# A PEER decoder block: the first product of tokens 0-511 in two passes over U, two token tiles each

## The chip, the cores and the metric

The kernel runs on one core of a Trainium2 chip. The metric is the device time of one execution in microseconds (us), from the first instruction to the last with the launch around them. All arithmetic that counts for the tables is done in float32, a value split into a high part (fp32r) and a low part.

## The reference, cut to what matters

One decoder layer over 1024 tokens of width 1024: attention and a convolution side by side, then a feed-forward part that looks experts up by product keys. The second part is what the change touches.

```python
q = (xb @ w_q).reshape(T, 8, 2, 128)             # 8 heads, two halves
s = einsum('thpc,hpkc->thpk', q, sub_keys)       # 128 keys for each half
top_s, top_i = top_k(s, 16)                      # 16 of 128, then the 16 best sums of pairs
...
ids = i1 * 128 + i2                              # 8 x 16 = 128 experts of 16384 for each token
g = softmax(best_s)
act = gelu(einsum('td,thkd->thk', xb, u_tab[ids]))
y = einsum('thk,thkd->td', g * act, v_tab[ids])  # then h + y, and a last norm
```

## The kernel before, in words

P = 128, D = 1024, DK = 8 chunks of the width, tokens in NT = 8 tiles of 128, HALF = 512 tokens = HT = 4 tiles. TensorE is PE, VectorE DVE, ScalarE ACT, GpSimd POOL, SyncE SP. Every engine's program is written out by hand and kept in order by counting semaphores; nothing is reordered at run time.

The first 785 us (mixing part, queries, key scores and their top 16) are the same in both kernels. Three stages follow.

**First product.** Tokens 0-511 are multiplied with all 16384 rows of U. U comes in NB = 32 blocks of 512 experts, each in two halves `hb` of KH = 4 chunks. For a half, SP loads 1 MB (`xraw<-in_uX`, L316, two slots), ACT rounds it (`hx`, L636), DVE takes the rest (`lx`, L1049), and PE does 4 chunks x 4 tiles x 3 products (L1426). After a block ACT copies four banks to `hst` (L642) and SP stores them to the DRAM tensor `hidden` (L322, 256 KB each). `load_x(hb)` waits for `lx_ready` of two halves earlier, and stands in SP's queue behind the stores of the block before. `high_u` waits until PE is through with the half two before.

Beside the first half of the blocks DVE finds the experts (`pick`, 14 steps for each of 8 tiles, PICK_STEPS = 4 steps for each half). PE turns the result of tiles 4-7 (L1403). Beside the second half the gates of tokens 512-1023 are spread out to a dense 128 x 128 matrix for each token, in 64 blocks of 8 tokens, two for each half: DVE `mark` (L1058), ACT `plain` (L669) and POOL `scale_hot` (L427) make one-hot operands, PE multiplies them (L1413, 16 small matmuls), ACT copies (`gather`, L662), SP writes `gates`, 16 times 2 MB (L326).

**Boundary.** Then POOL gathers from `hidden` the values that tokens 0-511 chose (L437, one instruction for each of the 512 columns), ACT applies Gelu (L709), DVE multiplies with the gate.

**Groups.** Tokens 512-1023 are computed densely over all experts, in NG = 32 groups of 4 blocks of 128 experts: first product (L1454, 96 matmuls, operands `uh`, `ul` from `u_raw`), Gelu (L730), times gate (L1121), second product (L1462, 96 matmuls), added to `acc` (L1141). For tokens 0-511 POOL gathers one row of V for each of the 512 columns (`gather_row`, L449, 512 KB, a ring of VS = 8 slots) and DVE adds it (`combine`, L1106), 16 rows in each group. POOL's order in a group is 8 rows, then 8 pairs of row and value, then 8 values:

```python
for c in range(NG):
    for j in range(PER_GROUP + VS):
        if j < PER_GROUP:
            gather_row(c * PER_GROUP + j)
        if j >= VS and c + 2 < NG:
            gather_value(c + 2, j - VS)
```

Of the kernel before, what the change touches and what calls it, by code (L numbers as in the profile page):

```python
# [5 lines left out]
P = 128  # L6
D = 1024
T = 1024
DK = D // P
# [24 lines left out]
BANKS = 4  # L34
# [9 lines left out]
PICK_STEPS = 4  # L44
PICKED = list(range(NT // 2, NT)) + list(range(NT // 2))
TURN_AT = [STEPS_PICK * (i + 1) // (2 * PICK_STEPS) for i in range(NT // 2)]
# [11 lines left out]
HOT_FROM = NB  # L58
HOTS = 2
# [34 lines left out]

def decoder_block(nc, x, xT, w_in, w_out, w_q, keysT, uT, uX, v_tab, consts, params, final_g, out):

    gates = nc.dram_tensor("gates", (NG, P, HALF // SUB, GC, SUB), F32, kind="Internal").ap()
    hidden = nc.dram_tensor("hidden", (HALF, PITCH), F32, kind="Internal").ap()
    hidden_items = hidden.rearrange("t (e o) -> (t e) o", o=1)
# [19 lines left out]
    with ctx:  # L119
# [48 lines left out]
        hst = at(HN + 16384, "hst", [P, HT, WIDTH])  # L168
# [21 lines left out]
        gbuf = [at(MID + 16384, "gbuf0", [P, NKEY, SUB]), at(16384, "gbuf1", [P, NKEY, SUB])]  # L190
        marks = [at(offset, f"marks{k}", [P, RAW // 2, 2, HOT // 2, NKEY, 2], BF16)
                 for k, offset in enumerate((MID + 131552, MID + 74208))]
# [3 lines left out]
        vring = [at(offset, f"vring{k}", [P, D]) for k, offset in enumerate(  # L196
            (HN + 8192, HN + 12288, HN + 16384, HN + 20480, MID + 16384, MID + 20480, MID + 127456, MID + 4096))]
        u_raw = at(HN, "u_raw", [P, 2, D])
        uh = at(HN + 24576, "uh", [P, 2, DK, P], F32R)
        ul = at(MID + 131552, "ul", [P, 2, DK, P], F32R)  # L200
        v_raw = at(MID + 8192, "v_raw", [P, VR, D])
        wh = at(MID + 24576, "wh", [P, GC, HALF], F32R)
        hg = at(MID + 32768, "hg", [P, 2, HALF])
        vh = at(MID + 40960, "vh", [P, GC, D], F32R)
        vl = at(MID + 57344, "vl", [P, GC, D], F32R)
        gt = at(MID + 74208, "gt", [P, HALF // SUB, GC, SUB])
        wl = at(MID + 82400, "wl", [P, GC, HALF], F32R)
        fg = at(MID + 123360, "fg", [P, D])
# [46 lines left out]
        hst_out = [sem(f"hst_out{n}") for n in range(HT)]  # L255
        best_ready, exp_ready, sel_ready, selT_ps, selT_ready = sems("best_ready exp_ready sel_ready selT_ps selT_ready")
        ids_ready = sem("ids_ready")
        el_in = sem("el_in")
        act_ready, wA_ready = sems("act_ready wA_ready")
        rows_out, rows_in = sem("rows_out"), [sem("rows_in0"), sem("rows_in1")]  # L260
# [26 lines left out]
        def _(sp):  # L287
# [23 lines left out]
            def load_x(hb):  # L311
                if hb >= 2:
                    sp.wait_ge(lx_ready, hb - 1)
                else:
                    sp.wait_ge(xl_ready, 2 * DK)
# [24 lines left out]
            for b in range(NB):  # L340
                for hb in (2 * b + 2, 2 * b + 3):
                    if hb < 2 * NB:
                        load_x(hb)
# [1217 lines left out]
```

## Time and profile before

| what | value |
|---|---|
| median of 3 runs | 3262.54 us (3254.13 to 3265.19) |
| the profiled execution's own time | 3263.35 us |
| its span, first to last instruction | 3261.5 us |
| PE busy | 2991.2 us (92%) |
| DVE busy | 2151.7 us (66%) |
| ACT busy | 980.6 us (30%) |
| POOL busy | 1501.1 us (46%) |
| moved by DMA | 617.11 MB, mean 189 GB/s |

Busy shares are means over the whole span. Matmuls overlap each other, so a stretch of PE that is called 100% busy is one without a gap. The granted clock stands beside it: 1.00 is the higher of TensorE's two levels, and 0.75 is a mixture of the two.

### The profile page before, as it was taken

The numbers are of one execution on the slowest core, as the hardware profiler recorded it, in microseconds if no ns is written. First come the engines' busy times: TensorE is split into PE (matmuls) and PEld (weight loads), VectorE is DVE, ScalarE is ACT, GpSimd is POOL, SyncE is SP. The second block draws the span as 40 slices with busy tenths as digits, with TensorE's granted clock in tenths as the row PEclk, the third lists the DMA queues.
The fourth block names the chain that finished last, engine by engine and source line by source line (L and its number), as shares of the span: only waits on it lengthen the run. The fifth ranks groups of instructions, "written<-read, shape, count | busy, mean of one in ns | idle before, by whom it ended". The sixth has DMA issues, their size and how long they took to land.

```text
span 3261.5 us, 34536 instructions
## 1 busy us (share of the span) xinstructions
PE 2991.2 (92%) x12784; PEld 2314.8 (71%) x12784; DVE 2151.7 (66%) x3502; ACT 980.6 (30%) x1300; POOL 1501.1 (46%) x1235
## 2 busy tenths in 40 slices
PE   7879689997999999999948999999999999999997
PEld 3435544786888888888836777777777777777776
DVE  1746953678777533333318778878878877877878
ACT  2003332211223245665522322222222222222222
POOL 2958500110000022222256676676676676667662
PEclk9989589998999999999979999999999999999999
DMA  3010110211343445545466877877877877877876
GB/s 117 33 39 1 52 39 1 84 40 71 130 155 127 144 142 194 170 172 181 163 224 253 319 268 258 315 269 261 315 271 252 316 278 258 308 272 260 306 277 232
DMA packets 234167, 617.11 MB, mean 189 GB/s; under 512 B 33424, under 2 KB 99088, under 8 KB 220944
## 3 DMA queue, kind: packets, MB, share of 16 engines
q1 hardware_dynamic: 143888, 346.15, 29.6%
q0 software_dynamic: 90112, 268.76, 22.9%
q8 instruction: 101, 1.65, 0.2%
q14 instruction: 66, 0.54, 0.1%
HBM read 539.32 MB, written 75.50 MB: 189 GB/s over the span
## 4 chain that ended last, share of the span: by engine, by line
PE 49%; DVE 18%; POOL 12%; DMA 11%; issue 7%; DVEq 1%; ACT 1%; SPq 0%; ACTq 0%; POOLq 0%
PE ps L1426 22%; POOL hsel L437 10%; DVE ps L1106 7%; PE ps L1454 6%; DMA vring<-in_v_tab,idsA 6%; PE ps L1385 6%; DMA u_raw<-in_uT 5%; PE ps L1222 3%; PE ps L1413 3%; PE ps L1313 3%; DVE hnT L791 3%; DVE ul L1085 2%; POOL vring L449 2%; PE ps L1182 1%; DVE vl L1116 1%
## 5 line engine op out<-in xcount | busy, mean ns | idle before, releaser
L1106 DVE SCALAR_TENSOR_TENSOR ps<-vring,hsel,ps 128x1024 f32<-128x1024 f32 x508 | 652.7, 1285 | 106.8 <-DMA vring<-in_v_tab,idsA 96.3
L449 POOL DMA_INDIRECT vring<-in_v_tab,idsA x512 | 561.9, 1097 | 349.9 <-DVE ps L1106 239.9
L437 POOL DMA_INDIRECT hsel<-hidden,idsE x512 | 522.6, 1021 | 172.5 <-issue 154.5
L1454 PE MATMUL ps<-xh,uh 128*128 128x512 f32 x1024 | 423.2, 413 | 114.5 <-DVE ul L1085 114.5
L427 POOL TENSOR_TENSOR hot<-marks,selG 128x1024 f32<-128x1024 bf16 x64 | 121.9, 1905 | 739.6 <-DVE marks L1058 406.1
L1426 PE MATMUL ps<-hx,xh 128*128 128x512 f32 x1024 | 407.0, 397 | 20.7 <-DVE lx L1049 20.7
L1049 DVE TENSOR_TENSOR lx<-xraw,hx 128x2048 fp32r<-128x2048 f32 x64 | 166.9, 2608 | 385.3 <-ACT hx L636 385.3
L1462 PE MATMUL ps<-vh,wh 128*128 128x512 f32 x1024 | 402.0, 393 | 18.8 <-DVE wl L1126 17.9
L1454 PE MATMUL ps<-xh,ul 128*128 128x512 f32 x1024 | 417.8, 408 | 0.0
L1454 PE MATMUL ps<-xl,uh 128*128 128x512 f32 x1024 | 416.7, 407 | 0.0
L1426 PE MATMUL ps<-lx,xh 128*128 128x512 f32 x1024 | 406.9, 397 | 0.0
L1462 PE MATMUL ps<-vh,wl 128*128 128x512 f32 x1024 | 405.1, 396 | 0.0
L1462 PE MATMUL ps<-vl,wh 128*128 128x512 f32 x1024 | 404.6, 395 | 0.0
L1426 PE MATMUL ps<-hx,xl 128*128 128x512 f32 x1024 | 404.5, 395 | 0.0
L1454 PEld LDWEIGHTS ps<-xh,uh 128*128 128x128 f32 x1024 | 201.3, 197 | 173.8 <-DVE ul L1085 111.4
L726 ACT CAST vh<-v_raw 128x1024 fp32r<-128x1024 f32 x128 | 133.9, 1046 | 581.9 <-PE ps L1462 581.9
L1462 PEld LDWEIGHTS ps<-vh,wh 128*128 128x128 f32 x1024 | 192.7, 188 | 69.3 <-DVE wl L1126 22.7
L1426 PEld LDWEIGHTS ps<-hx,xh 128*128 128x128 f32 x1024 | 193.5, 189 | 64.6 <-DVE lx L1049 20.9
L1454 PEld LDWEIGHTS ps<-xl,uh 128*128 128x128 f32 x1024 | 202.0, 197 | 48.1
L1454 PEld LDWEIGHTS ps<-xh,ul 128*128 128x128 f32 x1024 | 201.4, 197 | 48.9
L1462 PEld LDWEIGHTS ps<-vl,wh 128*128 128x128 f32 x1024 | 192.8, 188 | 46.2
L1426 PEld LDWEIGHTS ps<-lx,xh 128*128 128x128 f32 x1024 | 193.1, 189 | 41.6
(183 smaller groups left out, 4592.2 us busy)
## 6 DMA issues: line engine op xcount, KB each, us to landing
xraw<-in_uX SPq DMA_DIRECT2D x64, 1024.0 KB, 6.6
u_raw<-in_uT SPq DMA_DIRECT2D x128, 512.0 KB, 8.2
v_raw<-in_v_tab SPq DMA_DIRECT2D x128, 512.0 KB, 5.3
hidden<-hst SPq DMA_DIRECT2D x128, 256.0 KB, 2.1
gates<-gbuf SPq DMA_DIRECT2D x16, 2048.0 KB, 9.4
gt<-gates SPq DMA_DIRECT2D x32, 1024.0 KB, 7.0
wqbuf<-in_w_q SPq DMA_DIRECT2D x16, 512.0 KB, 3.4
hsel<-hidden,idsE POOLq DMA_INDIRECT x512
```

What stands on the lines that cost most here:

```text
L427: nc.gpsimd.tensor_tensor(hot[:, b % ROWS, 1, :, :].rearrange("p (c e) k -> p c e k", e=2), marks[b % RAW // 2][:, b % 2, 1, :, :, :].rear ...
L437: nc.gpsimd.indirect_dma_start(out=hsel[:, n, k:k + 1], out_offset=None, in_=hidden_items, in_offset=bass.IndirectOffsetOnAxis(ap=idsE[:, ...
L449: nc.gpsimd.indirect_dma_start(out=vring[q % VS][:, :], out_offset=None, in_=v_rows, in_offset=bass.IndirectOffsetOnAxis(ap=idsA[:, n, k:k ...
L726: nc.scalar.copy(vh[:, c, :], v_raw[:, c % VR, :]).then_inc(vh_ready, 1)
L791: nc.vector.scalar_tensor_tensor(out=y, in0=ubuf[:, c, bass.ds(k, T)], scalar=par[:, bass.ds(k + CW + c * TAPS, 1)], in1=y, op0=ALU.mult, ...
L1049: nc.vector.tensor_tensor(lx[hb % 2][:, :, :], xraw[:, hb % 2, :, :], hx[hb % 2][:, :, :].bitcast(F32), ALU.subtract).then_inc(lx_ready, 1)
L1106: nc.vector.scalar_tensor_tensor(out=bank2(6), in0=vring[j % VS][:, :], scalar=w, in1=bank2(6), op0=ALU.mult, op1=ALU.add).then_inc(cb_don ...
L1222: last = mm(ps[:, 2 * (blk % 2) + hb, :], w[:, k, :], wide[:, k, hb * 512:(hb + 1) * 512], start=k == 0, stop=k == DK - 1)
L1385: last = mm(ps[:, 2 * (m % 2) + half, :], w[:, m % 2, k, :], xx[:, k, :], start=k == 0 and xx is xh[half] and w is wqh, stop=k == DK - 1 a ...
L1426: last = mm(ps[:, n, :], w[:, k, n * P:(n + 1) * P], u[hb % 2][:, kk, :], start=k == 0 and w is xh[0] and u is hx, stop=k == DK - 1 and w ...
L1454: last = mm(ps[:, c % 2, :], w[:, c % 2, k, :], xx[:, k, :], start=k == 0 and w is uh and xx is xh[1], stop=k == DK - 1 and w is ul)
L1462: last = mm(ps[:, 2 + k % 4, :], w[:, c, tt * P:(tt + 1) * P], v[:, c, dh * 512:(dh + 1) * 512], start=c == 0 and w is wh and v is vh, sto ...
```

## The change

U is gone through twice. `H` counts 128 halves: H < 64 with tiles 0 and 1, then H >= 64 with tiles 2 and 3. `hidden` becomes two tensors, one for each pass. A half now holds 4 chunks x 2 tiles x 3 products. PSUM banks 0-3 are used two by two (`B % 2 * PT + n`), and the gate blocks keep 2 banks instead of 4.

The 112 steps of the picks are spread over the 64 halves of pass 1 (1.75 for each). In pass 2 stand: a gate block every HOT_SPAN = 3 chunks (halves 0 to 47 of the pass), 128 value gathers from pass 1's tensor (4 for each of the first 8 halves, then 2), their Gelu, and 96 of the 512 row gathers and additions (from half 12 of the pass; the first 8 rows are gathered from half 8 on). The groups keep 384 values and 416 rows: 13 or 14 rows for each of the first 31 groups and none in the last; rows and values alternate one by one.

Space: `marks` (now 4 blocks in one tensor), `gbuf0`, and others move. `marks` and `gbuf0` lie where `xh[1]` and `xl[1]` are, so SP stores these two (2 MB each) in pass 1 and loads them back when the gates are done. `acc` is reloaded in pass 2 too (2 x 2 MB), not in the first group.

```diff
-BANKS = 4
+BANKS = 2
-PICK_STEPS = 4
-PICKED = list(range(NT // 2, NT)) + list(range(NT // 2))
+PT = 2
+PICKED = [4, 0, 5, 6, 7, 1, 2, 3]
+HALVES = 2 * NB
+HOT_SPAN = 3
+EARLY_ROWS = 96
+EARLY_CHUNKS = 8
+ROWS_FROM = 12
...
+def picks_done(hb):
+    return min(NT * STEPS_PICK, NT * STEPS_PICK * (hb + 1) // HALVES)
+def share(total, parts, n):
+    return total * n // parts
...
 # SP
+            for B in range(2 * NB):
+                for H in (2 * B + 2, 2 * B + 3):
+                    if H < 2 * HALVES:
+                        load_x(H)
+                if B == 1:
+                    sp.dma_start(x_rows[0], xh[1][:, :, :].bitcast(F32)).then_inc(x_out, 16)
+                    sp.dma_start(x_rows[1], xl[1][:, :, :].bitcast(F32)).then_inc(x_out, 16)
+                store_hidden(B)
+                for m in range(HALF // SUB):
+                    if NB + (HOT_SPAN * SUB // HOT * (m + 1) - 1) // DK + 1 == B:
+                        write_gates(m)
+                if B == NB + HOT_SPAN * HT * BLOCKS // DK + 1:
...
+                    for half in (1, 0):
+                        sp.dma_start(acc[:, half * HT:(half + 1) * HT, :],
+                                     h_rows[:, half * HT:(half + 1) * HT, :]).then_inc(rows_in[half], 16)
+                    sp.wait_ge(hot_scaled, HT * BLOCKS + RAW)
+                    sp.dma_start(xh[1][:, :, :].bitcast(F32), x_rows[0]).then_inc(x_back, 16)
+                    sp.dma_start(xl[1][:, :, :].bitcast(F32), x_rows[1]).then_inc(x_back, 16)
...
 # POOL
+            for hb in range(HALVES):
+                for n in range(HT * BLOCKS):
+                    if (HOT_SPAN * n + 2) // KH == hb:
+                        scale_hot(n)
+                todo = values + (4 if hb < 8 else 2)
+                while values < min(todo, early_values):
+                    gather_value(values)
+                    values += 1
+                todo = 0
+                if hb >= ROWS_FROM:
+                    todo = VS + share(EARLY_ROWS, HALVES - ROWS_FROM, hb - ROWS_FROM + 1)
+                elif hb >= ROWS_FROM - VS // 2:
+                    todo = rows + 2
+                while rows < min(todo, EARLY_ROWS):
+                    gather_row(rows)
+                    rows += 1
+            for g in range(NG):
+                rows_end = EARLY_ROWS + share(HT * P - EARLY_ROWS, NG - 1, min(g + 1, NG - 1))
+                values_end = min(HT * P, early_values + (g + 1) * PER_GROUP)
+                while rows < rows_end or values < values_end:
+                    if rows < rows_end:
+                        gather_row(rows)
+                        rows += 1
+                    if values < values_end:
+                        gather_value(values)
+                        values += 1
...
 # ACT, pass 2
+            for hb in range(HALVES):
+                H = HALVES + hb
+                for kk in range(KH):
+                    n, r = divmod(hb * KH + kk, HOT_SPAN)
+                    if r == HOT_SPAN - 1 and n < HT * BLOCKS:
+                        gather(n)
+                        if n + ROWS < HT * BLOCKS:
+                            plain(*divmod(n + ROWS, BLOCKS))
+                if H % 2:
+                    for n in range(PT):
+                        evict(H // 2, n)
+                split_half(H + 2)
+                for c in range(EARLY_CHUNKS):
+                    if (6 + 4 * c if c < 2 else 2 + 8 * c) == hb:
+                        gelu_values(c)
...
 # DVE
+            for H in range(HALVES):
+                low_wide(H)
+                for k in range(picks_done(H - 1) if H else 0, picks_done(H)):
+                    pick(*divmod(k, STEPS_PICK))
+            dve.drain()
+            dve.wait_ge(x_out, 32)
+            marked = 0
+            for hb in range(HALVES):
+                low_wide(HALVES + hb)
+                while marked < min(HT * BLOCKS, KH * (hb + 1) // HOT_SPAN + 1):
+                    mark(*divmod(marked, BLOCKS))
+                    marked += 1
+                if hb >= ROWS_FROM:
+                    for q in range(share(EARLY_ROWS, HALVES - ROWS_FROM, hb - ROWS_FROM),
+                                   share(EARLY_ROWS, HALVES - ROWS_FROM, hb - ROWS_FROM + 1)):
+                        combine(q)
...
 # PE
+            def hidden_half(H):
+                B = H // 2
+                pe.wait_ge(lx_ready, H + 1)
+                for kk in range(KH):
+                    k = H % 2 * KH + kk
+                    for n in range(PT):
+                        t0 = (H // HALVES * PT + n) * P
...
+                    hot, r = divmod((H - HALVES) * KH + kk, HOT_SPAN)
+                    if 0 <= hot < HT * BLOCKS and r == HOT_SPAN - 1:
+                        hot_block(hot)
```

## Rows read from the trace of the kernel before

**Rows 1.** By stretch: length, busy of PE, PEld, DVE, ACT, POOL, clock, DMA share, GB/s

```profile
810.00:1169.00 359.00, 358.51 (x1549) 291.18 (x1550) 244.93 (x751) 100.51 (x112) 3.75 (x2) 0.99 0.41 139
1169.00:1639.00 470.00, 469.45 (x2561) 403.02 (x2559) 161.72 (x93) 278.46 (x288) 118.14 (x62) 1.00 0.51 172
1639.00:1742.00 103.00, 52.35 (x196) 41.53 (x197) 40.13 (x43) 17.21 (x23) 62.70 (x63) 0.75 0.65 235
1742.00:3245.00 1503.00, 1420.96 (x5948) 1137.08 (x5947) 1199.43 (x1270) 398.06 (x532) 1021.72 (x962) 0.98 0.77 280
...
812.00:1162.00 350.00, 350.00 (x1516) 284.27 (x1515) 240.39 (x746) 97.74 (x108) 0.00 (x0) 1.00 0.41 141
```

**Rows 2.** The chain that ended last, first product: start, length, what

```profile
1176.44 5.55 PE ps L1426 x24
...
1631.11 5.56 PE ps L1426 x24
```

**Rows 3.** Waits between 1760 and 3160: us in total, times, longest

```profile
DVE ps L1106 <- DMA vring<-in_v_tab,idsA: 90.6, 25, 5.1
...
PE ps L1454 <- DVE ul L1085: 72.9, 28, 4.0
```

**Rows 4.** POOL by line, 1760 to 3160: busy, mean ns, idle before

```profile
L449 POOL DMA_INDIRECT vring<-in_v_tab,idsA x458 | 501.8, 1096 | 283.2 <-DVE ps L1106 181.7 <-issue 101.5
L437 POOL DMA_INDIRECT hsel<-hidden,idsE x463 | 474.5, 1025 | 141.9 <-issue 140.4 <-ACT hsel L709 1.4
```

**Rows 5.** Timeline of POOL in one group: first and last of 8 values in a row

```profile
2171.77 0.95 POOL L437 DMA_INDIRECT hsel<-hidden,idsE  x1 [0.30 <-issue]
...
2180.52 1.43 POOL L437 DMA_INDIRECT hsel<-hidden,idsE  x1 [0.30 <-issue]
```

**Rows 6.** Timeline of PE at the boundary: matmuls that came after a wait

```profile
1654.96 0.77 PE L1454 MATMUL ps<-xh,uh 128*128 128x512 f32 x1 [16.52 <-DVE ul L1085]
1690.33 0.80 PE L1454 MATMUL ps<-xh,uh 128*128 128x512 f32 x1 [21.42 <-DVE ul L1085]
1721.15 0.79 PE L1462 MATMUL ps<-vh,wh 128*128 128x512 f32 x1 [13.26 <-DVE wl L1126]
```

**Rows 7.** Five lines one by one: shortest, median, longest ns, first and last start

```profile
L1049 DVE TENSOR_TENSOR lx<-xraw,hx x64: 2282/2293/3954, 808.2 to 1609.8; 128x2048 fp32r<-128x2048 f32 x64
...
L636 ACT CAST hx<-xraw x64: 1897/1911/1918, 786.7 to 1607.8; 128x2048 fp32r<-128x2048 f32 x64
...
L427 POOL TENSOR_TENSOR hot<-marks,selG x64: 1897/1897/2106, 1165.0 to 1623.9; 128x1024 f32<-128x1024 bf16 x64
...
L1058 DVE TENSOR_TENSOR marks<-selI,iota x64: 1211/1214/1226, 1162.5 to 1614.4; 128x2048 bf16<-128x2048 bf16 x64
...
L1106 DVE SCALAR_TENSOR_TENSOR ps<-vring,hsel,ps x508: 1275/1284/1293, 1691.9 to 3242.6; 128x1024 f32<-128x1024 f32 x170
```

**Rows 8.** DMA of 900 to 1150: queue (packets, MB, share), issues (count, KB, us to landing)

```profile
q1 hardware_dynamic: 10079, 35.77, 42.1%
...
xraw<-in_uX SPq DMA_DIRECT2D x23, 1024.0 KB, 5.5
```

**Rows 9.** Timeline of ACT, 1260 to 1330: start, length, instructions

```profile
1282.62 2.67 ACT L642 COPY hst<-ps 128x512 f32<-128x512 f32 x4 [1.45 <-PE ps L1426]
...
1286.98 2.11 ACT L662 COPY gbuf<-ps 128x512 f32<-128x512 f32 x2
```

**Rows 10.** DMA issues, 1200 to 1640: count, KB, median us to landing

```profile
gates<-gbuf SPq DMA_DIRECT2D x16, 2048.0 KB, 9.4
xraw<-in_uX SPq DMA_DIRECT2D x28, 1024.0 KB, 10.8
```

**Rows 11.** The page's queue of the gathers: packets, MB, share of the span

```profile
q0 software_dynamic: 90112, 268.76, 22.9%
```

**Rows 12.** GB/s of all queues in 40 slices of 812 to 860

```profile
GB/s 253 416 123 0 0 0 0 184 314 355 41 0 0 0 0 0 0 0 254 382 306 259 362 287 164 423 184 0 7 0 0 0 0 0 14 0 77 370 381 203
```

**Rows 13.** Timeline of DVE in the last group: three additions between two of L1141

```profile
3228.82 4.07 DVE L1106 SCALAR_TENSOR_TENSOR ps<-vring,hsel,ps 128x1024 f32<-128x1024 f32 x3
```

More of the change, by code:

```diff
@@ L418, in _, with scale_hot @@
                                         ALU.subtract).then_inc(wql_ready, 1)
-            pool.sem_inc(hot_scaled, RAW)
-            for n in range(HT * BLOCKS):
+            def scale_hot(n):
                 i, b = divmod(n, BLOCKS)
@@ L732, in group @@
                     nc.scalar.copy(wh[:, c, :], hg[:, c % 2, :]).then_inc(wh_ready, 1)
-                    if c == 1 and not last:
-                        gelu_values(g + 1)
+                    if c == 1 and g and EARLY_CHUNKS + g - 1 < NG:
+                        gelu_values(EARLY_CHUNKS + g - 1)
                     if c < 2:
@@ new lines, in _ @@
+            for H in range(HALVES):
+                low_wide(H)
[13 more added lines that the diff above has]
+                        combine(q)
@@ L1109, in group, with rows @@
-            def group(n, e, first=False, last=False):
-                g = e + n * (NG // HT)
-                fresh = isinstance(e, int) and e == 0
-                js = iter(range(PER_GROUP))
+            dve.wait_ge(h1_ready, 2 * NB * PT)
+            for half in range(2):
+                dve.wait_ge(rows_in[half], 16)
+            def group(g, last=False):
+                start, end = (EARLY_ROWS + share(HT * P - EARLY_ROWS, NG - 1, min(n, NG - 1)) for n in (g, g + 1))
+                steps = [share(end - start, GC + 8, n) for n in range(GC + 9)]
+                def rows(step):
+                    for q in range(start + steps[step], start + steps[step + 1]):
+                        combine(q)
@@ L1123, in group @@
                                             gt[:, :, c, :], ALU.mult).then_inc(w_ready, 1)
-                    combine(n, e, next(js), fresh and c == 0)
+                    rows(c)
                     dve.wait_ge(wh_ready, m + 1)
@@ L1127, in group @@
                                             ALU.subtract).then_inc(wl_ready, 1)
-                    if c == 3 and not last:
-                        weights(g + 1)
                     if c < 2:
@@ L1134, in group @@
                 for k in range(8):
-                    if k < 4 if last else k % 2 == 0:
-                        combine(n, e, next(js))
-                    if last and k < 4:
-                        combine(n, e, next(js))
                     dve.wait_ge(op_ready, g * 8 + k + 1)
@@ L1141, in group @@
                     nc.vector.tensor_tensor(dst, dst, ps[:, 2 + k % 4, :], ALU.add).then_inc(op_free, 1)
[L1142 to L1145 removed]
+                    rows(GC + k)
                     if last and k == 5:
                         dve.wait_ge(fg_in, 16)
[L1148 to L1152 removed]
+                        final_tiles(0, HT, 1)
             def final_tiles(n0, n1, roots):
```

337 lines of the change are left out of this document (143 added, 194 removed).

## The prediction

> **What bounds the kernel now.** I read the busy time by stretch first. In the two halves of the first product (359 and 470 us) PE has no gap: 358.5 and 469.5 us busy at clock 0.99 and 1.00 [rows 1]. The chain there consists of PE pieces alone: 24 matmuls in 5.55 us, 0.231 us each, and from 1176.44 to 1631.11 there are 63 such pieces, one every 7.33 us; the 1.78 us between two of them are a gate block [rows 2]. The other engines wait for PE.
>
> The groups are different. (3245 - 1742) / 31 = 48.5 us for a group [rows 1], while its 192 matmuls need 192 x 0.231 = 44.4 us [rows 2]. 4.1 us are lost in each. The waits say where: in 28.9 groups PE waits 72.9 us for `ul` (2.5 us a group), and DVE, which makes `ul`, waits 90.6 us for gathered rows [rows 3]. POOL isn't full: 32 gathers at 1.06 us with 0.30 between them are 43.5 of 48.5 us [rows 4]. Its order is what makes the ring run dry: eight values in a row take 10 us [rows 5], in which no row is asked for. The rest, some 1.6 us, is the clock (0.98) and small waits.
>
> The boundary is 103 us for one group [rows 1]. PE waits there 16.5, 21.4 and 13.3 us [rows 6]. The second and third wait are made by POOL: 32 values (32 x 1.25 = 40 us) stand ahead of the first row.
>
> **What the change leaves alone.** PE's work. Pass 1 has 64 halves of 5.55 us (355 us), pass 2 64 x 5.55 + 64 x 1.78 = 469 us [rows 2]. So a loss can only come as waits of PE, where before there were none. U is loaded and split twice: 64 more of L636 (1.91 us, ACT) and of L1049 (2.29 us, DVE) [rows 7] and 67 MB, all in half the time for each.
>
> **Pass 1: +30 us.** DVE holds a half 2.29 us for `lx`, and the picks took 240.4 - 32 x 2.29 = 167 us [rows 1, 7], 2.6 for each of 64 halves: 4.9 of 5.55 us. It fits on average, but a pick step can't be cut, and `lx` stands behind it. I take an estimate of 7 us for this, between 0 and half a microsecond in each half (32).
> The load of U is the tighter part. For two halves (11.1 us of PE) the way from the end of a block to the start of the one after next is: rest of the two `hst` copies (0.67 us each [rows 9]) 0.75; two stores issued ahead of the load, estimate 0.4; load 5.5 [rows 8]; `hx` 1.9; `lx` 2.3 [rows 7]; four hand-overs, estimate 0.4. That is 11.25 us. Traffic is 2.62 MB for each 11.1 us, 236 GB/s, against 139 before [rows 1], so I add 0.8 for the load: 12.05. The next block runs inside this time, so only half the excess is lost for each block: (12.05 - 11.1) / 2 x 32 = 15 us. Bounds: the load at 5.5 us (2 us) and at 10.8 us, its median beside the gates [rows 10] ((17.35 - 11.1) / 2 x 32 = 100 us).
> Saving `xh[1]` and `xl[1]`: 4.19 MB at 2.94 us for 1 MB (42.1% of 250 us for 35.77 MB [rows 8]) are 12.3 us ahead of one load, which has some 4 us of slack: 8. Bounds 0 and 12.
> 7 + 15 + 8 = 30, bounds 2 and about 144.
>
> **Pass 2: +96 us.** Two halves with gate blocks are 15.85 us of PE (11.1 + 8/3 x 1.78). Two of three blocks have a gate write of 2 MB in SP's queue just ahead of the next load. Before, such loads took 10.8 us [rows 10] and 29 us of PE hid them. Now: 0.75 + 0.4 + 10.8 + 0.4 as above, 1.9 for `hx`, 1.5 for gate copies that stand before it (2.11 us for two [rows 9], but not always in the way), 1.3 for a mark or an addition before `lx` (1.21 and 1.28), 3.0 for `lx` itself (2.29, up to 3.95 when POOL computes beside it [rows 7]): 20.05, 4.2 us too long. It is paid once in three blocks: 8 x 4.2 = 34 us.
> In 36 of the halves rows come too: 1.85 x 0.524 = 0.97 MB for each half, besides 1.05 (U), 0.26 (`hidden`) and 0.70 (gates): 2.98 MB. At 2.94 us for 1 MB of SP's queue and 22.9% x 3261.5 / 268.76 = 2.78 for POOL's [rows 11] they take 8.6 us of the 16 engines, PE 7.9. I take 3 us more landing for each of 6 threesomes: 18; bounds 0 and 36 x 1.7 (8.6 us at 90% of the engines less 7.9) = 59.
> Every third half ends with a gate block, and ACT then does two copies, a plain copy (estimate 1.1), in odd halves two evictions (1.3), and `hx` 1.9, and DVE `lx` 3.0: 9.2 against 7.33 us. 8 x 1.8 + 8 x 0.6 = 19; half of it falls into waits that I have counted: 10. Bounds 0 and 19.
> Last 16 halves (no gates, still 1.85 rows each): chain 14.05 with a load of 7: (14.05 - 11.1) / 2 x 8 = 12; bounds 0 and 30.
> `acc`, `xh[1]`, `xl[1]` come back as 8.4 MB right before a load: 8.4 x 2.94 = 24.7 us, of which I take 22; bounds 10 and 25.
> 34 + 18 + 10 + 12 + 22 = 96, bounds 10 and about 170. Check: all of pass 2 is 67.1 + 16.8 + 33.6 + 54.5 + 8.4 = 180.4 MB, 522 us at these rates, already 53 us over PE's 469.
> POOL in these 36 halves: 1.33 x 1.90 [rows 7] + 3.85 x 1.36 [rows 4] = 7.8 us of 7.9, so nearly full, but under the 8.9 to 9.5 us that the halves take by my sum; so it costs nothing more. Without that cover it is a rival, below.
>
> **Boundary: -47 us.** Rows and values run ahead, so the second and third wait go (34.7 us, and the low clock of 0.75 with them). The first stays in part: the loads of `u_raw` still wait for the last `hidden` store, but without 2 MB of gates ahead: 9.5 instead of 16.5 us. One group then takes 44.4 + 9.5 + 2 = 56 instead of 103. Bounds -25 and -55.
>
> **Groups: -98 us.** Rows and values alternate, at most three values follow each other, and DVE has 2.6 additions (3.3 us) less. I take 3.15 of the 4.1 us back, 31 times: the wait for `ul` (2.5) and a part of the clock. Bounds 0 (another wait takes its place) and 127 (all).
>
> **Tail: -4 us.** In the last group DVE has 3 additions (4.07 us) between two of L1141 [rows 13], against 2.77 us of PE for each; now it has none. Bounds 0 and -6.
>
> **Sum.** 30 + 96 - 47 - 98 - 4 = -23. The profiled execution took 3263.35 us (span 3261.5), 0.8 over the median. 3263.35 - 23 = **3240 us**.
>
> **A rule against the transfer terms.** The slices of a burst reach 416 and 423 GB/s [rows 12], above the 340 to 360 that the engines' packet times give, so the ceiling may be higher. The Trainium skill (DMA: Bandwidth & Descriptors, section Bandwidth) has 341 GB/s for a copy of 1 MB and 425 GB/s for 16 MB on one core; the slices agree. By it 180.4 MB take 424 us, less than PE's 469, and pass 2 wouldn't be bound by transfers: that is rival A. Its section Queues, rings and completion order says that an engine takes turns between queues packet by packet, which would lengthen a load behind gates while gathers are under way; no row here shows the two together.
>
> **Rivals.**
> *A, transfers stay hidden.* For it: the bursts [rows 12], and loads before were ready long before their use. Against it: SP's order puts gates and stores before the load. Then pass 1 costs 2 + 8, pass 2 19 + 26 (ACT's order, the reload): 3263 + 55 - 149 = 3169 us. Chance 0.20.
> *B, slower: loads of U land late everywhere.* Place: `load_x` behind stores, gates and gathers. Price for each microsecond of mean landing beyond mine: 16 us in pass 1, 4 in the last halves, about 5 at the gates. It decides from 1 us more on (23 us / 25). With a landing of 8.5 us in pass 1, half way to 10.8, it gives 35 + 9 + 19 = 63 more: 3303 us. Chance 0.27.
> *C, POOL's gathers.* A gather beside DVE's 2.3 us `lx` may take twice as long (mean 1.10 [rows 4], 0.95 alone [rows 5]). With 0.6 us more for each, 3.85 gathers bring POOL to 10.1 us a half, 0.9 over my halves, 36 times, and 12 of the values-only halves likewise: about 45 more, 3285 us. Against it: 1.06 on average in the groups beside a DVE that is 80% busy [rows 1, 4]. Chance 0.05.
> *D, the groups stay at 47.5 us or more.* PE waits for `ul` with its chain Gelu, gate, addition, `ul`, about as long as the 5.55 us of a block even if no row is late. Gain 31 instead of 98: 3307 us. Chance 0.06.
> *Forecast as summed*, 3205 to 3275: 0.42.
>
> **Chances and range.** 0.3% is 10 us, about what a measurement of this kernel can tell from no change. Forecast: 0.30 faster, 0.10 same, 0.02 slower. A: 0.20 faster. B: 0.02 faster, 0.02 same, 0.23 slower. C and D: 0.01 faster, 0.01 same, 0.09 slower. Faster 0.53, same 0.13, slower 0.34. The range goes from A's 3169 to just over B's and D's, 3165 to 3325; the forecast's own is 3205 to 3275.
>
> **What the new profile would show.** Pass 1 (about 389 us): PE with short waits for `lx`, DVE near 90% busy; if the waits lead back to `xraw<-in_uX` the load is the cause, if to picks the step sizes. Pass 2 (about 566 us): PE waits for `lx` after blocks with a gate write, landing of `xraw` over 10 us, DMA share near 0.9. First group near 56 us, the others near 45.3 with no DVE wait for `vring`. I am wrong if PE in pass 2 has no gaps (A), or if pass 1 takes over 420 us (B), or if DVE waits for rows in the passes (C), or if a group still takes over 47 us (D).

## The result, and the profile after

The changed kernel takes 3302.49 us (median of 4, 3301.80 to 3306.22) where the kernel before took 3263.86 (median of 4): ratio 1.0125, 95% interval 1.0100 to 1.0149. It is slower by some 39 us; forecast were 23 us less.

The first view is the busy time by stretch, the same as in [rows 1]: length, busy of PE, PEld, DVE, ACT, POOL, then the granted clock, DMA share and GB/s. Pass 1 is 810 to 1191, pass 2 is 1191 to 1857, the first group 1857 to 1914, the other 31 groups 1914 to 3290.

```profile
810.00:1191.00 381.00, 367.39 (x1548) 292.54 (x1549) 313.34 (x781) 158.45 (x143) 0.00 (x0) 0.98 0.67 231
1191.00:1495.00 304.00, 247.39 (x1267) 208.51 (x1266) 161.12 (x98) 175.89 (x173) 220.38 (x149) 0.90 0.70 240
1495.00:1700.00 205.00, 164.99 (x847) 140.37 (x846) 122.27 (x81) 116.68 (x116) 137.74 (x97) 0.87 0.77 269
1700.00:1857.00 157.00, 111.09 (x451) 87.86 (x449) 78.70 (x52) 45.38 (x42) 71.89 (x59) 0.86 0.87 321
1857.00:1914.00 57.00, 48.53 (x204) 39.36 (x205) 37.04 (x40) 15.84 (x20) 24.79 (x23) 0.94 0.73 254
1914.00:3290.00 1376.00, 1376.00 (x5942) 1114.71 (x5940) 1106.02 (x1178) 401.34 (x533) 800.15 (x762) 1.00 0.78 269
```

Against [rows 1], stretch by stretch: pass 1 381 us for 359 (+22), pass 2 666 for 470 (+196), first group 57 for 103 (-46), 31 groups 1376 for 1503 (-127, 44.4 us each). The tail behind them is 10.6 us for 16.5 (-6). These make +39, as the spans do (3300.6 and 3261.5). So four of these five stretches went as forecast or better, and pass 2 ate all of it and more.

In pass 2 PE is busy 247.39 + 164.99 + 111.09 = 523.5 us, where the same work took 469.45 at clock 1.00 [rows 1]. So 54 of the 196 us are matmuls that run slower, at a granted clock of 0.86 to 0.90 (a mixture of TensorE's two levels, after PE had begun to have gaps), and 142.5 us are the gaps themselves. The waits between 1191 and 1795 (us in total, times, longest) say what ended most of them:

```profile
ACT hx L682 <- DMA xraw<-in_uX: 113.8, 16, 29.3
...
PE ps L1480 <- DVE lx L1100: 88.4, 16, 21.5
ACT gbuf L708 <- DMA gates<-gbuf: 79.2, 7, 13.2
...
PE ps L1466 <- ACT gbuf L708: 40.2, 7, 8.9
```

The first two I had forecast: U lands late, `hx`, `lx` and PE follow. The last two I had not: ACT stands 79.2 us before gate buffers that are still being written out, 11.3 us each time, and PE's gate blocks stand behind it. Up to 1857 PE's waits before `lx` come to 93.9 us. With 40.2 before gate blocks for ACT and 7.6 before gate blocks for POOL (experiment 2 has that wait) they are the 142 us. The DMA issues between 1240 and 1650 (count, KB, median us to landing) give the landing times, to set beside [rows 10]:

```profile
xraw<-in_uX SPq DMA_DIRECT2D x36, 1024.0 KB, 12.3
gates<-gbuf SPq DMA_DIRECT2D x13, 2048.0 KB, 11.1
hidden<-hst SPq DMA_DIRECT2D x38, 256.0 KB, 2.6
```

U lands in 12.3 us (10.8 before), the gate write in 11.1 (9.4 before). A landing time starts at the issue, though, and the issue itself is late. One turn of it, in SP's timeline:

```profile
1449.08 0.82 SPq L344 DMA_DIRECT2D hidden<-hst  x2
1449.94 0.61 SPq L349 DMA_DIRECT2D gates<-gbuf  x1
1450.60 7.87 SPq L337 DMA_DIRECT2D xraw<-in_uX  x2
1474.68 0.81 SPq L344 DMA_DIRECT2D hidden<-hst  x2
1475.54 0.46 SPq L349 DMA_DIRECT2D gates<-gbuf  x1
1476.04 7.33 SPq L337 DMA_DIRECT2D xraw<-in_uX  x2
```

and in the same microseconds in those of ACT, DVE and PE, one after the other:

```profile
1464.51 1.87 ACT L708 COPY gbuf<-ps 128x512 f32<-128x512 f32 x2 [13.17 <-DMA gates<-gbuf]
...
1467.73 1.90 ACT L682 CAST hx<-xraw 128x2048 fp32r<-128x2048 f32 x1 [0.50 <-DMA xraw<-in_uX]
```

```profile
1469.66 2.29 DVE L1100 TENSOR_TENSOR lx<-xraw,hx 128x2048 fp32r<-128x2048 f32 x1 [13.66 <-ACT hx L682]
```

```profile
1465.67 3.63 PE L1466 MATMUL ps<-hot 128*128 128x128 f32 x16 [8.88 <-ACT gbuf L708]
```

The gate write that ends ACT's wait is the one of 1449.94: it lands at 1464.5, 14.6 us later. Its buffer had been full since 1416.8, when ACT's last copy into it ended, so 33.1 us went by before the write was issued. SP's program has it so. `write_gates(m)` stands behind the stores of the block after the one in which the buffer is filled, and these stores wait for that block's end. For every second buffer that is 12 chunks after its last gate block, for the others 8: 23.8 and 15.85 us at PE's full pace, where a block of U, 8 chunks, takes 15.85. ACT wants the same buffer again 15 chunks after it was full, 29.7 us at that pace (34.5 here, 1416.8 to 1451.3). With 11 us under way the write needs 35 us in the one case and 27 in the other, so every second write should be late. The trace has it so: of the 14 buffers that are filled again ACT waits for 7, every second one. In the kernel before SP issued a write right behind the last copy (at 1318.45 and 1347.78, the copies ended at 1318.43 and 1347.76), the next four gate blocks took 4 x 7.33 = 29 us [rows 2], and PE had no gap.

ACT's wait (13.17 us at 1464.51) holds PE's gate block (8.88 us). DVE's 13.66 us before `lx` have another cause, since the `hx` that it waits for begins at 1467.73 because its half of U lands then (the 0.50 of that row). That load was issued at 1450.60 right behind the gate write, and took 17.1 us. So the gate write harms twice: its buffer comes free late, and the load of U behind it lands late (in experiment 1, with the write out of the way, these loads land in 8.1 us in the median, not 12.3). In the chain that ended last, from 1191 to 1857, loads of U are 38.6% and gate writes 3.8%.

Of the groups the waits from 1914 to 3290 have no line of DVE that waits for `vring` any more, which [rows 3] had with 90.6 us. POOL waits for DVE instead, so the ring is full:

```profile
POOL vring L477 <- DVE ps L1145: 336.7, 181, 4.6
```

### The profile page after: what moved, and what is told of

The parts are those of the page before. It is cut to its first block, busy times and chain, and to the rows that moved or that the text cites. A ratio compares the mean times of both kernels' runs of the same rounds, so it can differ in the third digit from the quotient of the medians.

```text
span 3300.6 us, 34830 instructions
## 1 busy us (share of the span) xinstructions
PE 3004.7 (91%) x12784; PEld 2324.9 (70%) x12784; DVE 2318.8 (70%) x3565; ACT 1095.7 (33%) x1363; POOL 1549.5 (47%) x1235
## 4 chain that ended last, share of the span: by engine, by line
PE 74%; DMA 10%; DVE 8%; ACT 4%; issue 2%; DVEq 2%; SPq 0%; ACTq 0%
PE ps L1511 22%; PE ps L1519 21%; PE ps L1480 13%; DMA xraw<-in_uX 9%; PE ps L1438 6%; PE ps L1275 3%; PE ps L1366 3%; DVE hnT L842 3%; ACT hx L682 2%; PE ps L1466 2%; DVE lx L1100 1%; PE ps L1235 1%; PE ps L1330 1%; PE ps L1424 1%; DMA gates<-gbuf 1%
## 5 line engine op out<-in xcount | busy, mean ns | idle before, releaser
L477 POOL DMA_INDIRECT vring<-in_v_tab,idsA x512 | 542.7, 1060 | 553.6 <-DVE ps L1145 461.5
L469 POOL DMA_INDIRECT hsel<-hidden,idsE x512 | 576.3, 1125 | 149.2 <-issue 148.5
L1100 DVE TENSOR_TENSOR lx<-xraw,hx 128x2048 fp32r<-128x2048 f32 x128 | 315.2, 2463 | 348.0 <-ACT hx L682 347.2
L1480 PE MATMUL ps<-hx,xh 128*128 128x512 f32 x1024 | 429.1, 419 | 128.2 <-DVE lx L1100 127.9
L1511 PE MATMUL ps<-xh,uh 128*128 128x512 f32 x1024 | 404.0, 395 | 9.0 <-DVE ul L1123 9.0
L1511 PE MATMUL ps<-xl,uh 128*128 128x512 f32 x1024 | 402.6, 393 | 0.0
L456 POOL TENSOR_TENSOR hot<-marks,selG 128x1024 f32<-128x1024 bf16 x64 | 136.0, 2127 | 511.8 <-DVE marks L1109 510.9
L682 ACT CAST hx<-xraw 128x2048 fp32r<-128x2048 f32 x128 | 244.4, 1910 | 318.5 <-DMA xraw<-in_uX 253.5
L1206 DVE TENSOR_TENSOR acc<-acc,ps 128x512 f32<-128x512 f32 x256 | 175.4, 686 | 131.0 <-PE ps L1519 130.9
L1480 PEld LDWEIGHTS ps<-hx,xl 128*128 128x128 f32 x1024 | 201.2, 197 | 47.6
## 6 DMA issues: line engine op xcount, KB each, us to landing
gates<-gbuf SPq DMA_DIRECT2D x16, 2048.0 KB, 11.3
```

The lines of the kernel that those rows point to most:

```text
L456: nc.gpsimd.tensor_tensor(hot[:, b % ROWS, 1, :, :].rearrange("p (c e) k -> p c e k", e=2), marks[:, b % RAW, 1, :, :, :].rearrange("p c k ...
L469: nc.gpsimd.indirect_dma_start(out=hsel[:, n, k:k + 1], out_offset=None, in_=hidden_items[n // PT], in_offset=bass.IndirectOffsetOnAxis(ap ...
L477: nc.gpsimd.indirect_dma_start(out=vring[q % VS][:, :], out_offset=None, in_=v_rows, in_offset=bass.IndirectOffsetOnAxis(ap=idsA[:, n, k:k ...
L682: nc.scalar.copy(hx[H % 2][:, :, :], xraw[:, H % 2, :, :]).then_inc(hx_ready, 1)
L1100: nc.vector.tensor_tensor(lx[hb % 2][:, :, :], xraw[:, hb % 2, :, :], hx[hb % 2][:, :, :].bitcast(F32), ALU.subtract).then_inc(lx_ready, 1)
L1206: nc.vector.tensor_tensor(dst, dst, ps[:, 2 + k % 4, :], ALU.add).then_inc(op_free, 1)
```

## The experiments

Nine kernels ran. Where rounds aren't named, a time is one execution, and that of the kernel before on the same chip stands beside it (its median, where it has several). Executions of one kernel lie up to 16 us apart (3185.96 to 3201.68 in experiment 8), so smaller differences between single times show nothing by themselves. Experiments 1 to 4 ran on one chip, 5 to 7 on a second, 8 and 9 on a third. The length of pass 2 is in all of them the time from 1191 us to the start of the last matmul of the hidden product: 665 us in the changed kernel (1856.1). Pass 2 begins up to 3 us before or after 1191, and the lengths are uncertain by that much. The expectations have it rounded otherwise in places, by 1 us.

### 1. Gate writes from ACT's queue

The write is issued by ACT right behind the last copy into the buffer, and no longer by SP behind the stores.

```diff
 # SP
-                for m in range(HALF // SUB):
-                    if NB + (HOT_SPAN * SUB // HOT * (m + 1) - 1) // DK + 1 == B:
-                        write_gates(m)
 # ACT, gather(n)
+                if n % (SUB // HOT) == SUB // HOT - 1:
+                    act.wait_ge(gp_free, (n + 1) * HQ + BANKS)
+                    act.dma_start(gates[:, :, m, :, :].rearrange("g p c t -> p g (c t)"),
+                                  gbuf[m % 2][:, :, :].rearrange("p (g c) t -> p g (c t)", c=GC)).then_inc(gates_out[m % 2], 16)
```

> The changed kernel with one edit: the 16 gate writes of 2 MB are issued from ScalarE's own DMA queue, right behind the copies of their last block, and not from SP's queue behind the hidden stores and ahead of the next loads of U. The changed kernel's pass 2 took 666 us (1191 to 1857), 469 of them PE's work. Theory Q (queue order: a load of U stands behind 2 MB, and the write itself comes late, so that ACT waits for its buffer): pass 2 falls to 540-590 us, the whole to about 3200 us. Theory T (traffic: the 16 engines are simply busy, whatever the order): pass 2 stays within 20 us of 666, the whole at 3285-3305.

Measured: 3245.87 us (before: 3266.84). Pass 2 is 606 us, 59 less than in the changed kernel, though it moves the same bytes. Theory T is refuted. Theory Q has the direction, but both its ranges were too low (540-590 and about 3200). The waits of pass 2 have no line of `gbuf` waiting for `gates` left. DMA issues, 1240 to 1650:

```profile
xraw<-in_uX SPq DMA_DIRECT2D x42, 1024.0 KB, 8.1
gates<-gbuf ACTq DMA_DIRECT2D x14, 2048.0 KB, 17.3
hidden<-hst SPq DMA_DIRECT2D x42, 256.0 KB, 5.8
```

The gate write is slower now (17.3 for 11.1 us) and harms nobody; U is faster (8.1 for 12.3), and a store of `hidden` slower (5.8 for 2.6). The queues share the engines. The Trainium skill (DMA: Bandwidth & Descriptors, section Queues, rings and completion order) says that an engine takes turns between its queues packet by packet. These three rows agree with a sharing; no run here shows the size of a turn. What counts here is that an order in time became a sharing: the transfer that nobody waits for took the delay.

The edit mends two things at once, the late issue of the write and the load of U behind it. PE's waits say what each is worth together with the clock: before gate blocks for ACT 40.2 us become 0, before `lx` 93.9 become 70.0, PE's busy time falls from 523.5 to 508.0 us (less of it at the lower clock), and against these its waits for POOL grow from 7.6 to 27.1.

### 2. Gate writes of 1/32 of the bytes

The kernel leaves out the gates of groups 1 to 31: each write brings those of group 0 alone (64 KB), and every group reads these. The place in SP's queue stays.

```diff
-                sp.dma_start(gates[:, :, m, :, :].rearrange("g p c t -> p g (c t)"),
-                             gbuf[m % 2][:, :, :].rearrange("p (g c) t -> p g (c t)", c=GC)).then_inc(gates_out[m % 2], 16)
+                sp.dma_start(gates[0:1, :, m, :, :].rearrange("g p c t -> p g (c t)"),
+                             gbuf[m % 2][:, 0:GC, :].rearrange("p (g c) t -> p g (c t)", c=GC)).then_inc(gates_out[m % 2], 16)
-                sp.dma_start(gt[:, :, :, :], gates[g]).then_inc(g_in, 16)
+                sp.dma_start(gt[:, :, :, :], gates[0]).then_inc(g_in, 16)
```

> The changed kernel with each gate write cut to 1/32 of its size (the first group's gates alone), and every group reading those; what is left out: the gates of groups 1 to 31. It removes 32.5 MB of pass 2's 180 and keeps every wait. Theories Q and T both: pass 2 falls by over 90 us, to 540-580, and ACT no longer waits for its gate buffer. If pass 2 stays over 620 us, neither is the cause, but the order of ACT's and DVE's work around a gate block, or the 8.4 MB that are loaded back.

Measured: 3231.46 us (before: 3266.84), pass 2 591 us, U's landing 6.8 us. Without the gates' bytes 74 us go, less than the 90 that both theories asked for; ACT's waits for the gate buffer fall to 14.4 us. 59 of the 74 went in the first experiment too, with all bytes there. So with the rows in place the order makes most of the gates' cost and the bytes 15 us.

What keeps pass 2 from falling further is a wait that the profile doesn't name:

```profile
PE ps L1466 <- issue: 37.4, 15, 4.1
```

The one-hot operand that PE's gate block needs comes from POOL (`scale_hot`, here L456). One of the 15 waits, in POOL's timeline and in PE's:

```profile
1466.87 3.75 POOL L456 TENSOR_TENSOR hot<-marks,selG 128x1024 f32<-128x1024 bf16 x2
```

```profile
1468.87 2.82 PE L1466 MATMUL ps<-hot 128*128 128x128 f32 x16 [3.43 <-issue]
```

The first of POOL's two ends at 1468.8, PE starts 0.1 us later, and so it is with all 15: each ends 0.09 to 0.13 us after a `scale_hot`. POOL was late because four gathers of the half before, two values and two rows, stood ahead of it in its program and took from 1459.3 to 1466.9. In the changed kernel such waits are 7.6 us (3 times), in experiment 1 27.1 (11 times). They grow as the other waits go.

### 3. No row sums in pass 2

```diff
-EARLY_ROWS = 96
+EARLY_ROWS = 0
```

> The changed kernel with EARLY_ROWS = 0: no row gathers or additions in pass 2, 16 or 17 in each of the first 31 groups. Theory Q: pass 2 falls by 20-50 us, since only the landing of loads gets shorter. Theory T: by 100 us or more (50 MB of 180 gone). Groups: if alternating rows and values is what filled them, they stay at 44.4-45.5 us each and the whole is near 3260 us; if it was the 2.6 additions fewer, they go up to 47 us or more (80 us more in all).

Measured: 3259.33 us (before: 3266.84). Pass 2 is 619 us, 46 less, within theory Q's 20-50 and far from theory T's 100. The groups, which now do all 512 rows, take some 5 us more, so it wasn't the smaller number of additions that filled them. By these single times the 96 early rows were a net loss of 43 us. The gate buffer's wait stays:

```profile
ACT gbuf L708 <- DMA gates<-gbuf: 62.0, 7, 9.0
```

### 4. The kernel before with rows and values in turn

Are the groups faster because rows and values alternate, or because 16 values and 3 rows fewer for each group are left? The kernel before, with POOL's order alone changed (and two semaphores for the values, so that a chunk's arrival is counted by itself):

```diff
-            for c in range(NG):
-                for j in range(PER_GROUP + VS):
-                    if j < PER_GROUP:
-                        gather_row(c * PER_GROUP + j)
-                    if j >= VS and c + 2 < NG:
-                        gather_value(c + 2, j - VS)
+            for q in range(HT * P):
+                gather_row(q)
+                v = q + 2 * PER_GROUP - VS
+                if q >= VS and v < HT * P:
+                    gather_value(*divmod(v, PER_GROUP))
```

> The kernel before with one edit: in the groups POOL gathers one row and one value in turn, in place of 8 rows, 8 pairs and 8 values in a row; two semaphores for the values, so that a chunk need not wait for Gelu of the one before. One pass over U as before, 16 rows in each group. If the run of 8 values is what emptied the ring: the wait for ul goes, a group takes 44.5-46 us and the whole 3165-3200 us. Rival: 32 gathers at 1.36 us fill POOL (43.5 of 44.4 us), a group takes 47-48 us and the whole 3230-3260.

Measured: 3357.16 us (before: 3266.84), 90 us slower, where I had expected a gain. ACT's Gelu of the values now waits in every group:

```profile
ACT hsel L709 <- DMA hsel<-hidden,idsE: 196.0, 31, 7.9
```

Value q + 24 goes with row q, so the 16 values whose Gelu stands early in ACT's group are complete only when POOL is in the middle of that group. Behind that Gelu on ACT stands `uh`, from which PE's next operands are made (PE waits 177.8 us for `ul`, 31 times). The experiment changed two things, the order and the values' lead, so it doesn't answer the question.

### 5. The same with a lead for the values

```diff
             gather_values(0)
-            gather_values(1)
...
+            v = PER_GROUP
+            for q in range(HT * P):
+                gather_row(q)
+                for _ in range(2 if q < PER_GROUP else 1):
+                    if v < HT * P:
+                        gather_value(*divmod(v, PER_GROUP))
+                        v += 1
```

> The kernel before, rows and values in turn as in before_alternating, but with the values of the next group 16 further ahead: after the first 16 values, two values for each of the first 16 rows, then one for one with value q + 32 beside row q. before_alternating took 3357 us: ACT waited 196 us for values at Gelu, 31 times, so my reading is that the values had no lead left. If that is so, ACT's wait is gone, PE's wait for ul with it, a group takes 44.4-45.5 us and the whole 3130-3170 us. Rival: POOL is full with 32 gathers at 1.36 us; then PE waits, a group takes 46-48 us, the whole 3190-3250.

Value q + 32 goes with row q, so the values are 8 rows further ahead than in experiment 4 (not 16), and as far ahead as in the kernel before, where POOL ends a group with the values of the next but one.

Measured, 3 rounds: **3124.75 us** (3123.97 to 3132.62; before: 3265.19), ratio 0.9585, interval 0.9561 to 0.9609. That is 5 us below the range. By stretch:

```profile
1169.00:1637.00 468.00, 468.00 (x2554) 401.84 (x2553) 161.83 (x93) 276.48 (x285) 118.06 (x62) 1.00 0.50 171
1637.00:1742.00 105.00, 65.53 (x267) 52.42 (x266) 51.16 (x55) 25.19 (x33) 77.69 (x76) 0.80 0.80 275
1742.00:3100.00 1358.00, 1358.00 (x5860) 1099.57 (x5859) 1184.83 (x1253) 391.79 (x522) 985.01 (x949) 1.00 0.88 306
```

The first product is as before, without a gap. The boundary isn't better than [rows 1] has it (105 for 103). The groups run like those of the changed kernel, without a gap of PE at clock 1.00, though they have all 16 rows and 16 values each: the second product's first to last matmul take 1402 us (1703.9 to 3106.1), 1400 in the changed kernel (1888.9 to 3289.3) and 1541 in the kernel before (1703.3 to 3244.6). So POOL's order, with the lead kept, is enough for all that the change gains in the groups. It needs no second pass over U. Experiment 4 had the same order without the lead; the lead alone is worth 3357.16 - 3124.75 = 232 us.

### 6. Gate writes by ACT and no rows in pass 2

Experiments 1 and 3 together.

> gates_by_act with EARLY_ROWS = 0 as well. gates_by_act alone left pass 2 at 606 us, no_early_rows alone at 618. Theory Q (order): the order being mended, rows add only a little, pass 2 falls to 585-600 us. Theory T (traffic, as the DMA share of 0.91 of gates_by_act between 1550 and 1700 suggests): now that order is mended the engines are the limit, and 50 MB less give 550-570 us. The groups then have 16 or 17 rows and stay at 45.2 us each, as in no_early_rows: the whole 3190-3245 us.

Measured: 3205.65 us (before: 3265.19, median of 7). Pass 2 is 565 us: 100 less than in the changed kernel, where the two edits singly gave 59 and 46, so the terms nearly add up. Theory T's range (550-570) holds and theory Q's doesn't. But traffic is not the whole of the 41 us by which it is under experiment 1: PE's waits for POOL fall from 27.1 to 8.3 us, those before `lx` from 70.0 to 58.5, its busy time from 508.0 to 498.0. Its waits still have

```profile
ACT hx L679 <- DMA xraw<-in_uX: 81.8, 15, 30.7
```

### 7. Gate writes and the reload from ACT's queue

`acc`, `xh[1]`, `xl[1]` come back in ACT's queue at half 51 of the pass, beside SP's loads of U and not ahead of one; the block that did it in SP's program is gone, and ACT's has the same waits. Rows are as in the changed kernel, gate writes as in experiment 1.

```diff
 # ACT, ahead of the half
+                if hb == 51:
...
+                    for half in (1, 0):
+                        act.dma_start(acc[:, half * HT:(half + 1) * HT, :],
+                                      h_rows[:, half * HT:(half + 1) * HT, :]).then_inc(rows_in[half], 16)
+                    act.wait_ge(hot_scaled, HT * BLOCKS + RAW)
+                    act.dma_start(xh[1][:, :, :].bitcast(F32), x_rows[0]).then_inc(x_back, 16)
+                    act.dma_start(xl[1][:, :, :].bitcast(F32), x_rows[1]).then_inc(x_back, 16)
```

> gates_by_act, and the 8.4 MB that are loaded back (acc, xh[1], xl[1]) issued from ScalarE's queue too, so that loads of U don't stand behind them. In gates_by_act PE waits about 25 us there in one piece. If the order is the cause: that wait shrinks to under 10 us, pass 2 580-590, the whole 3220-3230 us. If the bytes are: two or three smaller waits take its place, and the whole stays at 3240-3248.

Measured: 3238.70 us, 7 less than experiment 1 (a single time on another chip); pass 2 599 for 606. Neither theory's numbers hold. PE's longest wait falls from 25.20 us (experiment 1, first row) to 16.78 (second):

```profile
1731.03 0.80 PE L1481 MATMUL ps<-hx,xh 128*128 128x512 f32 x1 [25.20 <-DVE lx L1101]
```

```profile
1725.06 0.80 PE L1481 MATMUL ps<-hx,xh 128*128 128x512 f32 x1 [16.78 <-DVE lx L1101]
```

Two thirds of the wait stay. All waits of PE before `lx` from 1700 to the end of the pass are 21.5 us for 30.1. Between 1690 and 1780 the DMA engines are 97% busy, which speaks for the bytes as the price of what is left.

### 8. All three mended

Gate writes and reload from ACT's queue, no rows in pass 2.

> All three terms of the second pass mended at once: gate writes and the reload issued from ACT's queue, no row sums in either pass (they run in the 31 groups). Gate writes by ACT without rows gave 3205.65 us with a second pass of 564 us; the reload by ACT took 8 us off the second pass when the rows were there (606 to 598). Theory (terms add): second pass about 556, time 3198 (range 3193 to 3204). Rival (the reload costs about 25 in its own wait, and without rows it goes wholly): second pass about 540, time 3182. Second rival (with the rows away nothing is late behind the reload, so it costs nothing and moving it gains nothing): 3206. If it stays above 3170 in every case, two passes over U remain behind the single pass with values and rows in turn (3124.75), by the first product's length alone.

Measured, 5 rounds: 3191.31 us (3185.96 to 3201.68; before: 3262.28), ratio 0.9776, interval 0.9763 to 0.9789. Pass 2 is 556 us, 9 less than in experiment 6, as the sum of the terms had it. Moving the reload gives 7 to 9 us with rows or without, neither 25 nor nothing, by single profiles; PE's waits in them agree (the longest falls from 26.32 us in experiment 6 to 13.87). The time is 7 us below the terms' 3198 and 2 below their range; the profiled execution is the slowest of the five, so the single execution of experiment 6 may have been one too. The best form of two passes that I ran is 67 us behind experiment 5 (3191.31 - 3124.75).

### 9. Small gate writes and no rows

Experiments 2 and 3 together; again the gates of groups 1 to 31 are left out.

> The changed kernel without its row sums and with gate writes cut to 1/32 of their bytes (it leaves out the gates of groups 1 to 31: every group reads those of group 0). The gate write stays in SP's queue behind the stores of hidden. Without rows, gate writes whole and by SP: second pass 618 us; whole and by ACT: 564. Theory (ACT waits for its gate buffer because the write is issued and lands late; a small write lands soon even from SP's queue, and the 16 MB are gone too): second pass 550 to 565, time 3190 to 3207. Rival (it is the place in SP's queue behind the stores that makes the write late, whatever its size): second pass about 600, time 3240.

Measured, 3 rounds: 3157.75 us (3156.11 to 3161.44), ratio 0.9680, interval 0.9665 to 0.9695. Pass 2 is 517 us, shorter than either theory had it. The small write issued behind SP's stores hardly stops ACT any more (first fence, 10.4 us in 7 waits, for 79.2 in the changed kernel and 62.0 in experiment 3), and the clock is back near 1.00 until the reload (second fence: 1191 to 1495 and 1495 to 1600, in the columns of the first view):

```profile
ACT gbuf L708 <- DMA gates<-gbuf: 10.4, 7, 1.6
```

```profile
1191.00:1495.00 304.00, 295.08 (x1645) 252.56 (x1644) 154.63 (x86) 230.09 (x225) 239.76 (x139) 0.98 0.47 158
1495.00:1600.00 105.00, 104.22 (x579) 88.35 (x578) 48.20 (x27) 77.91 (x75) 77.19 (x46) 1.00 0.53 179
```

In these 409 us PE lacks 10 us in all. Of the last 109 it lacks 27, nearly all in one wait at the reload:

```profile
1650.62 0.80 PE L1480 MATMUL ps<-hx,xh 128*128 128x512 f32 x1 [25.47 <-DVE lx L1100]
```

## Why the prediction was wrong

**Pass 1, +30.** Right; measured +22. PE's busy time of 367.39 of 381 shows short waits, DVE at 313.34 is below the 90% that I gave. The waits that are new come to 13 us, 7.2 of them in one piece at 852.8, after the saving of `xh[1]` and `xl[1]` (8 forecast); some 9 us are slower matmuls. So the saving was right, and picks and late loads together cost less than their 7 + 15.

**Pass 2, +96: this step failed.** Measured +196. The terms that failed are *gates 34* and *rows 18*. Together 52 us, they measure 665 - 517 = 148:

| pass 2, us | gate writes by SP | by ACT | small |
|---|---|---|---|
| 96 rows | 665 | 606 | 591 |
| no rows | 619 | 565 | 517 |

PE's time in each of the six splits like this (us; what is missing to the length is up to 3 us of waits for ACT's operand and rounding). PE's same work is 469.45 us busy at clock 1.00 [rows 1]:

| pass 2 | length | PE busy | waits before `lx` | for a gate buffer | for POOL's `scale_hot` |
|---|---|---|---|---|---|
| 96 rows, by SP | 665 | 523.5 | 93.9 | 40.2 | 7.6 |
| 96 rows, by ACT | 606 | 508.0 | 70.0 | 0 | 27.1 |
| 96 rows, small | 591 | 503.1 | 48.1 | 0 | 37.4 |
| no rows, by SP | 619 | 517.7 | 61.3 | 32.0 | 7.6 |
| no rows, by ACT | 565 | 498.0 | 58.5 | 0 | 8.3 |
| no rows, small | 517 | 480.9 | 28.0 | 0 | 6.6 |

*Gates*: with the rows gone 619 - 517 = 102 us instead of 34 (the small write leaves the copies and the waits, and takes away nearly all bytes): 33 before `lx`, 32 for the gate buffer, 37 of slower matmuls. Of the 102, 54 are the place in SP's queue (619 - 565) and 48 the bytes (565 - 517); with the rows there the place is worth 59 and the bytes 15. My 4.2 us for every third block priced the load of U that stands behind the write, and at a landing of 10.8 us, where the loads in the chain between 1250 and 1480 took 13.0 to 17.1. I gave no price to the write itself: its issue comes 24 to 37 us after its buffer is full, ACT wants the late ones again after 34 to 39 us, and ACT, which waits for it, holds PE's gate block. That two-buffer loop is the wait that I missed. It is 40.2 us of PE's waits in the changed kernel, and experiment 1 takes it to nothing with all bytes still moved. How the rest of the place's cost divides between the loop and the load of U behind the write no run shows: issuing the write from SP one block earlier, which would mend the first alone, was not tried.

*Rows*: 46, 41 and 74 us, column by column, instead of 18; my upper bound was 59. The table takes them apart. Before `lx` they cost 33, 12 and 20 us, for POOL's `scale_hot` 0, 19 and 31, in slower matmuls 6, 10 and 22, and 8 for the gate buffer in the first column. The part for `scale_hot` lies in POOL's program, where the row gathers stand ahead of it, and not in the landing of bytes. It also says why gates' bytes and rows don't add up (over 517 the bytes alone cost 48, the rows alone 74, both 89): with the rows there, taking the bytes away takes 22 us off the waits before `lx` and puts 10 on those for POOL.

*The other three terms* (ACT's order, the last halves and the reload, 10 + 12 + 22 = 44) agree with what stays in experiment 9, 517 - 470 = 47, but as a sum that is luck. The reload is right: 25.47 us in its one wait. The others are 11.5 us of slower matmuls, which I had no term for, 8.2 at gate blocks (6.6 of them for POOL), and 2.5 in all further waits before `lx`. For the last halves experiment 9 is no test, since it has no rows in them.

The slow clock isn't a term of mine at all: 54 of the 196 us. It isn't a cause of its own, since it comes with the gaps and goes with them (0.86 to 0.90 in the changed kernel, 0.98 and 1.00 in experiment 9), but a sum in microseconds at full pace leaves it out.

**First group, -47.** Right; -46. PE waits 8.98 us at its start, 9.5 forecast, and no second or third time.

**Groups, -98.** Sign right, size too small: -127, my upper bound, all 4.1 us of each. I had kept 1 us a group for the clock and small waits; without the wait for `ul` these went too. Experiment 5 confirms the mechanism (the order of the gathers) and shows that the two passes aren't needed for it; by experiment 3 the smaller number of additions isn't either.

**Tail, -4.** Measured -6.

**The rivals.** *A* (transfers hidden) is refuted by PE's gaps. *B* named the sign, the place (`load_x` behind stores and gates) and 3303 us, and half of the mechanism: U did land late in pass 2 (12.3 us in the median for my 10.8 at the gates). But 35 of its 63 us were to come from pass 1, which was fine, and it has no wait for the gate buffer. That its time agrees is chance: pass 2 cost 100 more than forecast and the groups 29 less. *C*: in pass 2 a row's gather takes 1.11 us and a value's 1.32 in the mean, 0.01 and 0.29 over the groups' of [rows 4] and not 0.6, and POOL is 430 us busy of 666. So its price was wrong and in the changed kernel POOL costs PE 7.6 us. Its place was right, though: once the gate write is mended, PE waits 27.1 and 37.4 us for POOL in experiments 1 and 2. That POOL "costs nothing more" held only while other waits covered it. *D*: groups take 44.4, not 47.5.

**Still open.** How much of the rows' part before `lx` is their traffic and how much DVE's additions ahead of `lx` and of the marks. And whether pass 2 falls further with `scale_hot` ahead of the gathers in POOL's program, or with the gate write issued a block earlier: neither was run.

## What to carry to other kernels

For each buffer that a queue drains, write down the whole loop (full, issued behind which waiting instruction, landed, wanted again): a landing time starts at the issue and doesn't show the first part, and a queue where the transfer is issued at once can be worth more than its bytes. Try a reordering alone in the old kernel before work is doubled to make room for it; POOL's order gave 4.15% by itself (experiment 5), while the second pass over U, as changed here, cost more than it freed, and its best form (3191.31 us) stayed 67 us behind. Change an order with each stream's lead kept: without it the same order cost 90 us. Where a wait has no name in the profile, look which engine's result came just before its end: the next limit may stand there already.

## What the hardware showed that I had not expected

- A write of 2 MB on ACT's queue beside SP's loads and POOL's gathers lands in 17.3 us (11.1 on SP's queue), and the loads of U in 8.1 (12.3): whoever shares is slowed, and one can choose who.
- In experiment 7 all three queues together moved 378 GB/s over the 90 us from 1690 to 1780, with slices of 2.25 us up to 451 GB/s. My 2.94 us for 1 MB is 340 GB/s, so as a limit it was some 10% too strict.

```profile
DMA packets 7714, 34.02 MB, mean 378 GB/s; under 512 B 1181, under 2 KB 1773, under 8 KB 5785
```

- The groups of experiment 5 keep PE without a gap while the DMA engines are 88% busy at 306 GB/s for 1358 us. A high share was no sign of a bound there (my reading is that U and V were asked for early enough; no run tests it); in pass 2 of the changed kernel a share of 0.70 to 0.77 went with 97 us of gaps in 509.
